# The recurrence's keys by token: from three TensorE transposes a head to VectorE blocks and transfers inside SBUF

## What is computed

```
b = jnp.cumsum(fn, axis=2)
inter = jnp.einsum('bhtk,bhkv->bhtv', qn * jnp.exp(b), state)
...
o = inter + jnp.einsum('bhts,bhsv->bhtv', a, vn)
b_last = b[:, :, -1:, :]
state = (jnp.exp(b_last[:, :, 0, :])[..., None] * state
         + jnp.einsum('bhsk,bhsv->bhkv', kn * jnp.exp(b_last - b), vn))
```

## Time and profile before

| | |
|---|---|
| median of 3 runs | 2543.14 us (2542.96 to 2543.50) |
| the profiled execution, its own time | 2543.12 us |
| its span, first to last instruction | 2541.8 us |
| TensorE busy | 2529.5 us, 100% |
| VectorE / ScalarE busy | 1355.3 us (53%) / 942.6 us (37%) |
| granted TensorE clock, mean | 0.999 |
| mean traffic of transfers | 122 GB/s |

### The profile page before, as it was taken

How to read it: one execution, slowest core, us unless ns; L and a number is a source line. 1 busy time by engine, 2 the same in 40 slices (tenths; PEclk the granted TensorE clock), 3 DMA queues, 4 the chain that set the end, 5 groups by cost and what they waited for, 6 DMA issues and landing times.

```text
span 2541.8 us, 31922 instructions
## 1 busy us (share of the span) xinstructions
PE 2529.5 (100%) x13178; PEld 2101.0 (83%) x13178; DVE 1355.3 (53%) x2215; ACT 942.6 (37%) x1298; POOL 77.9 (3%) x64
## 2 busy tenths in 40 slices
PE   9999999999999999999999999999999999999998
PEld 8888888888888888888888888888888888888888
DVE  7547743468544555655442363684365445554425
ACT  6543335333332222222332353543344344444323
POOL 0000000000000000000000102200000000000000
PEclk9999999999999999999999999999999999999999
DMA  5322333322335666666453233335322322222434
GB/s 190 115 84 84 91 93 100 92 84 84 92 97 166 214 217 203 222 219 212 132 174 99 84 108 95 88 100 184 91 67 74 91 75 83 79 81 86 167 94 158
DMA packets 159986, 309.32 MB, mean 122 GB/s; under 512 B 11040, under 2 KB 15392, under 8 KB 158816
## 3 DMA queue, kind: packets, MB, share of 16 engines
q1 hardware_dynamic: 159040, 305.70, 39.0%
q0 software_dynamic: 224, 1.15, 0.1%
q10 hardware_dynamic: 576, 0.42, 0.1%
HBM read 298.84 MB, written 8.39 MB: 121 GB/s over the span
## 4 chain that ended last, share of the span: by engine, by line
PE 100%; DVE 0%; ACT 0%; issue 0%
PE bank L341 94%; PE bank L1364 1%; PE bank L1363 1%; PE bank L1362 1%; PE bank L1528 1%; PE bank L762 0%; PE bank L835 0%; PE bank L746 0%; PE bank L838 0%; PE bank L795 0%; PE bank L1702 0%; DVE X L2107 0%; PE bank L1815 0%; PE bank L433 0%; PE bank L438 0%; PE bank L439 0%
## 5 line engine op out<-in xcount | busy, mean ns | idle before, releaser
L341 PE MATMUL bank<-XH,WH 128*128 128x512 f32 (+1 forms) x2880 | 1109.2, 387 | 0.0
L341 PE MATMUL bank<-XH,WL 128*128 128x512 f32 (+1 forms) x2880 | 1102.3, 385 | 0.0
L341 PE MATMUL bank<-XL,WH 128*128 128x512 f32 (+1 forms) x2880 | 1101.4, 384 | 0.0
L391 DVE TENSOR_TENSOR WL<-RAW,WH 128x1024 fp32r<-128x1024 f32 x443 | 546.3, 1234 | 761.4 <-ACT WH L368 760.5
L368 ACT CAST WH<-RAW 128x1024 fp32r<-128x1024 f32 x443 | 465.9, 1053 | 1067.2 <-PE bank L341 1063.3
L341 PEld LDWEIGHTS bank<-XH,WL 128*128 128x128 f32 x2880 | 540.7, 188 | 108.7 <-DVE WL L391 0.3
L341 PEld LDWEIGHTS bank<-XH,WH 128*128 128x128 f32 x2880 | 541.0, 188 | 106.6 <-issue 0.5
L341 PEld LDWEIGHTS bank<-XL,WH 128*128 128x128 f32 x2880 | 541.0, 188 | 106.0 <-issue 0.5
L341 PE MATMUL bank<-WH,XH 128*128 128x512 f32 x384 | 150.0, 391 | 0.0
L341 PE MATMUL bank<-WL,XH 128*128 128x512 f32 x384 | 149.5, 389 | 0.0
L341 PE MATMUL bank<-WH,XL 128*128 128x512 f32 x384 | 149.4, 389 | 0.0
(11 more groups left out here) (311 smaller groups left out, 1773.8 us busy)
## 6 DMA issues: line engine op xcount, KB each, us to landing
RAW<-in_w_in SPq DMA_DIRECT2D x303, 512.0 KB, 3.7
AST<-in_w_ada SPq DMA_DIRECT2D x192, 256.0 KB, 4.1
RAW<-in_w_out SPq DMA_DIRECT2D x40, 512.0 KB, 3.8
RAW<-in_w_o SPq DMA_DIRECT2D x32, 512.0 KB, 3.8
RAW<-in_w_gate SPq DMA_DIRECT2D x32, 512.0 KB, 3.8
RAW<-in_w_a SPq DMA_DIRECT2D x16, 512.0 KB, 4.3
RAW<-in_w_b SPq DMA_DIRECT2D x16, 512.0 KB, 4.4
XT<-in_xT SPq DMA_DIRECT2D x4, 1024.0 KB, 7.0
```

The lines of the kernel that those rows point to most:

```text
L341: ins = nc.tensor.matmul(bank[b][:, cols], l, r[:, cols], start=first, stop=final)
L391: nc.vector.tensor_tensor(WL[:, m % NSPL], RAW[:, m % NRAW], WH[:, m % NSPL].bitcast(F32), ALU.subtract).then_inc(lo.sem, lo.step(m))
```

## The change

The three transposes on TensorE and the copy on ScalarE go. VectorE turns KEYS in 32x32 blocks into a new buffer ZK right after it has made KEYS; ZK lies on the bytes of ST, so it waits for the output products of the head before. SP gets specials of its own: for each head it waits for ZK, then issues 16 transfers from SBUF to SBUF that put the blocks in place, each of 32 partitions with 3 runs of 128 bytes (12 KB). `chunk_sums` waits for the last of them. The pieces of TensorE and ScalarE keep their number.

```diff
@@ hgrn_pe
-        def keys_by_token(b):
-            T.wait_ge(dve, (yield dve, ("keys", hh)))
-            T.wait_ge(ld["idn"], (yield ld["idn"], 0))
-            for c in range(3):
-                ins = nc.tensor.transpose(b[:, CH[c]], KEYS[:, CH[c]], IDN[:, :])
-            ins.then_inc(side.sem, side.step(("kt", hh)))
-
         def chunk_sums(b):
             for j in range(4):
                 T.wait_ge(ev_a, (yield ev_a, (("iv", half), j)))
-            T.wait_ge(act, (yield act, ("kt", hh)))
+            T.wait_ge(keys_turned, (yield keys_turned, hh))
...
-        yield
-        b, was = special_bank(("kt", hh), act, ("kt", hh))
-        T.wait_ge(was[0], (yield was))
-        yield from keys_by_token(b)
-        yield
-        yield
+        yield from idle(3)
@@ hgrn_act
-        yield
-        yield
-        yield
-        A.wait_ge(side, (yield side, ("kt", hh)))
-        if hh:
-            A.wait_ge(side, (yield side, ("sums", hh - 1)))
-        nc.scalar.copy(KT[:, :, :], bank[banks["kt", hh]][:, 0:384].rearrange("p (c t) -> p c t", c=3)
-                       ).then_inc(act.sem, act.step(("kt", hh)))
-        yield
-        yield
-        yield
+        yield from idle(6)
@@ hgrn_dve
         if hh:
-            V.wait_ge(side, (yield side, ("kt", hh - 1)))
+            V.wait_ge(dve, (yield dve, ("kt", hh - 1)))
         nc.vector.tensor_tensor(KEYS[:, BEFORE_END], kk[:, BEFORE_END], EE[:, 1, BEFORE_END], ALU.mult
                                 ).then_inc(dve.sem, dve.step(("keys", hh)))
+        if hh:
+            V.wait_ge(side, (yield side, ("av", hh - 1)))
+        V.wait_ge(dve, (yield dve, ("keys", hh)))
+        nc.vector.transpose(ZK[:, :, :], KEYS[:, BEFORE_END].rearrange("p (b x) -> p b x", x=32)
+                            ).then_inc(dve.sem, dve.step(("kt", hh)))
         yield
+    def hgrn_sp(hh):
+        yield from idle(8)
+        Y.wait_ge(dve, (yield dve, ("kt", hh)))
+        if hh:
+            Y.wait_ge(side, (yield side, ("sums", hh - 1)))
+        for sj in range(4):
+            for ti in range(4):
+                nc.sync.dma_start(KT[32 * sj:32 * sj + 32, :, 32 * ti:32 * ti + 32], ZK[32 * ti:32 * ti + 32, sj:12:4]
+                                  ).then_inc(keys_turned.sem, keys_turned.step(*([hh] if sj == ti == 3 else [])))
+        yield
+        yield from idle(8)
@@ sp
         for half in range(2):
-            for name in ("fl", "q", "iv", "cg", "xa", "bg", "za"):
+            yield from sp_dense(("fl", half))
+            yield from turns.finish(turns.specials)
+            yield from sp_dense(("q", half))
+            yield from sp_dense(("iv", half))
+            for i in range(4):
+                turns.specials.append(hgrn_sp(4 * half + i))
+            for name in ("cg", "xa", "bg", "za"):
                 yield from sp_dense((name, half))
         yield from sp_dense(("og", 0))
         yield from sp_dense(("og", 1))
+        yield from turns.finish(turns.specials)
```

More of the change, by code:

```diff
@@ L276, in build @@
     stored = Signal(nc, "out_stored", 16)
+    keys_turned = Signal(nc, "keys_turned", 16)
     spilled = Signal(nc, "x3_spilled", 16)
@@ L495, in build @@
     ST = sb("ST", [3, 128], F32, W0 + 89856)
+    ZK = sb("ZK", [12, 32], F32, W0 + 89856)
     KEYS = sb("KEYS", [512], F32, W0 + 91392)
```

## The result

| | before | after |
|---|---|---|
| median | 2543.20 us (4 runs, 2542.96 to 2543.50) | 2562.68 us (4 runs, 2561.81 to 2565.01) |
| profiled execution, span | 2543.12, 2541.8 us | 2561.81, 2560.5 us |
| mean granted TensorE clock | 0.999 | 0.997 |

The ratio is 1.0079 (95% interval 1.0066 to 1.0091): the kernel became 19.5 us, or 0.8%, slower. The forecast was 2545.1, its range 2540.3 to 2557.0, with 0.60 on no change. The result lies above the range.

The account below looks back on a forecast made before the run. TensorE, never idle in the stretch, was taken as the bound: 2543.1 us, less 2.8 for the transposes, plus 4.8 of stalls (2 x 2.2 + 4 x 0.1), gave 2545.1 us; range 2540.3 to 2557.

Parts of the forecast that it names:

- What bounds the kernel, and what can be won: TensorE is busy throughout; removing its transposes wins 0.355 us a head, 2.8 us over 8 heads, and nothing more.
- VectorE: One block transpose of 128x384 float32 a head, right after KEYS, taken at 0.55 us.
- SP, the step that failed: Sixteen issues a head at 0.51 us spacing, so the last starts 7.65 us after the first.
- My upper bound of 0.67: SP's spacing at most some 0.67 us, from an issue at the start taking 0.63 once transfers pile up, plus its gap.
- Landing: From SP's issue to data in KT 1.5 us, the middle of 0.8 and 2.3.
- the six heads at the edge: All heads but 0 and 4: stalls forecast at 2.2 us in heads 2 and 6, 0.1 in the four odd ones.
- The dates: Last landing against TensorE's chunk sums: head 0 has 2.5 us to spare, odd heads 0.1; head 2 waits 2.0, stalling 2.2.
- a sign of being wrong: The forecast would be wrong if TensorE waited in heads 0 and 4 too, among other signs.
- The slow-issue rival: SP's sixteen issues spaced 0.65 us: stalls 4.3 in heads 2 and 6, 2.0 in odd heads; 2556.9 us; chance 0.26.
- The clock, a term left out of the sum: Rival: TensorE's clock falls in a stall, costing a few us for each fall; chance 0.02.
- The queue behind: Weight loads behind SP's pieces slip, but 9 us remain before ScalarE's cast in head 2; cost nothing.

Follow-up runs that it names:

- the run on the shapes: The kernel before with unread transfers inside SBUF added in heads 0 to 3, of 32 or 128 partitions, one or three runs each; 2542.99 us beside 2543.32.
- the run on the places: The kernel before with unread transfers added in heads 0 to 3, from HBM, from SBUF to HBM and inside SBUF; 2542.72 us beside 2542.91.

## Why the prediction was wrong

- **What bounds the kernel, and what can be won**: right. The floor is 2.7 us below, forecast 2.8.
- **VectorE**: right. 0.578 against 0.55.
- **SP, the step that failed.** "I take 0.51, as 12 KB pieces don't pile up." Measured: 0.64 from start to start (0.60 and 0.04), and up to 0.68 on average in heads in which single issues were longer (up to 1.23 us); what made those longer no run shows. Fifteen spacings are 9.6 to 10.2 us, not 7.65. The rows I leaned on were transfers out of HBM, and no row of the kernel before had both ends in SBUF. My upper bound of 0.67 held the usual value, but the forecast, and 0.60 of the chances, stood on the lower one.
- **Landing**: 1.8 against 1.5, within my ends of 0.8 and 2.3. It is 0.3 for each of the six heads at the edge. The Trainium skill's page "DMA: Bandwidth & Descriptors" with its fixed 2.0 us ("Anatomy of one DMA"), which it fits to transfers issued from GpSimd, was a little nearer to SP's 1.8 than my middle. Its rule that transfers under 512 bytes are read, modified and written ("Specifications") leaves no mark that these runs can tell: runs of 128 bytes land after 1.8 us here (2.4 in the run on the shapes), and in the run on the places transfers inside SBUF with runs of 1536 bytes, which carry more in all, land after 2.3.
- **The dates.** The order was right: least in heads 0 and 4, most in 2 and 6, because VectorE reaches KEYS late there. The sizes: 4.0 us in place of 2.2, some 2.1 in the odd heads in place of 0.1, and 0.2 and 0.3 in heads 0 and 4, which had 2.5 to spare in my sum and whose waiting I had named as a sign of being wrong. Fifteen spacings at 0.64 take 2.0 of that, the landing 0.3, and the longer single issues about the rest. The slow-issue rival had written 4.3, 2.0 and none; its waits sum to 16.6, and 16.8 were measured. It was given 0.26.
- **The clock, a term left out of the sum.** The same rival gave 2556.9, and my range ended there, since the fall of the clock was put down as a rival by itself with 0.02. It is no rival of the waits: it comes with them and adds to them. It fell at both waits of 4.03 us in the changed kernel, and at all six waits of 4.3 us and over in the one with twenty transfers. Some 4 us of the 19.5 are this. Without it the bill would stand at 2557.1, at the very end of the range; the spacing took the time there, and the clock took it past.
- **The queue behind**: right. Loads slipped, no cast waited for them.

The verdict flipped on a small number: with six heads on the edge, 0.13 us an issue, fifteen times a head, cost nearly 12 us, and twelve issues instead of sixteen bring the time back to 2543.5.

## What to carry to other kernels

Where many small steps in a row feed an engine that never idles, work out the date of the last one against the date at which it is wanted, in the latest of the repeats, and trust a "hidden" only if it stands for the worst price of the step. Count issues, not bytes: sixteen transfers inside SBUF cost 10 us of one queue, while the same sixteen on two queues, five transfers by way of HBM or sixteen 0.27 us copies on an engine with room hid the same work. And an edit whose whole prize is 0.1% is worth making only where no wait can come of it; once TensorE stands still, its clock may charge as well.

## What the runs showed of the hardware that I had not expected

- An issue on SP's queue in a row of them took, in the median, 0.59 to 0.63 us with both ends in SBUF, in all five shapes tried. With one end in HBM it took 0.42 to 0.43 for three kinds of small transfers, and 0.62 for a load of 12 runs of 128 bytes a partition. Issued from ScalarE's queue at the same time, eight inside SBUF took 5.55 us beside SP's 5.87.
- The length of a wait alone doesn't tell whether TensorE's clock falls. It fell to 0.50 at waits of 4.0 us and, in the kernel with the sums two pieces later, after both of 1.9 us; in the changed kernel four waits of about 2 us in the odd heads and in the one with twelve transfers two of 1.5 us left it at 1.00. With twenty transfers it fell after one of 2.57 and not after one of 2.68.
- ScalarE moves a 32x96 float32 block to another group of partitions in 0.269 us.
